# Feed-forward layers of a three-layer transformer on one core: eight block products per step replaced by seven, with the block sums made on GpSimd

## What is computed

```
def swiglu(x, w_gate, w_up, w_down):
    return (jax.nn.silu(x @ w_gate) * (x @ w_up)) @ w_down
x = x + 0.5 * swiglu(rms_norm(x, ffn1_norm), w_gate, w_up, w_down)   # 1024 -> 2816 (2752 in layer 3) -> 1024
x = x + mixer(rms_norm(x, mix_norm))     # pool + latent attention, gated convolution, Fourier + attention
x = x + 0.5 * swiglu(rms_norm(x, ffn2_norm), ...)
```

## Time and profile before

| | us |
|---|---|
| median of 3 runs | 2809.5 (2809.46 to 2810.23) |
| the profiled execution | 2811.45 |
| its span, first to last instruction | 2809.6 |
| PE busy | 2766.3 (98%) |
| DVE busy | 1331.8 (47%) |
| ACT busy | 908.2 (32%) |
| POOL busy | 130.3 (5%) |

### The profile page before, as it was taken

The page is one execution under the profiler, slowest core; times in us unless marked ns, Lnnn a source line. Parts: engine busy times, 40 slices in busy tenths (PEclk is TensorE's granted clock), DMA queues, the critical chain, the costliest instruction groups (busy, mean ns, idle before and its releaser), DMA issues.

```text
span 2809.6 us, 31389 instructions
## 1 busy us (share of the span) xinstructions
PE 2766.3 (98%) x12580; PEld 2261.5 (80%) x12580; DVE 1331.8 (47%) x1895; ACT 908.2 (32%) x1286; POOL 130.3 (5%) x130
## 2 busy tenths in 40 slices
PE   8999999999999999999999999999999999999998
PEld 6888878888888888888888888888877877788776
DVE  5444358654443444434654444344443557544432
ACT  4222226542322223222233232223222346432221
POOL 0000005300000000000000000000000114000000
PEclk9999999999999999999999999999999999999999
DMA  4332232033323333333333333333322320233322
GB/s 152 99 98 91 91 86 77 24 89 103 95 92 96 96 98 90 101 96 96 98 90 98 98 90 98 92 95 91 105 85 89 92 81 23 61 103 100 90 84 70
DMA packets 282704, 253.30 MB, mean 90 GB/s; under 512 B 8384, under 2 KB 278848, under 8 KB 282560
## 3 DMA queue, kind: packets, MB, share of 16 engines
q1 hardware_dynamic: 282560, 251.30, 29.9%
HBM read 249.17 MB, written 2.10 MB: 89 GB/s over the span
## 4 chain that ended last, share of the span: by engine, by line
PE 82%; issue 13%; DVE 3%; ACT 2%; DMA 0%; SPq 0%; POOLq 0%; POOL 0%; DVEq 0%
PE bank L380 27%; PE bank L381 27%; PE bank L382 27%; PE bank L469 1%; DVE a_mx L1235 0%; PE bank L433 0%; PE bank L422 0%; DMA raw<-in_ffn_w_gate 0%; DVE wl L1126 0%; ACT Xh L804 0%; DVE a_nb L1142 0%; ACT wh L773 0%; DVE a_KT L1138 0%; ACT a_P L857 0%; DVE X L1135 0%
## 5 line engine op out<-in xcount | busy, mean ns | idle before, releaser
L1126 DVE TENSOR_TENSOR wl<-raw,wh 128x1024 fp32r<-128x1024 f32 (+6 forms) x498 | 573.9, 1166 | 976.2 <-ACT wh L773 975.3
L380 PE MATMUL bank<-Xh,wl 128*128 128x512 f32 x2544 | 997.6, 392 | 12.9 <-DVE wl L1126 10.6
L382 PE MATMUL bank<-Xh,wh 128*128 128x512 f32 x2544 | 992.0, 390 | 0.0
L381 PE MATMUL bank<-Xl,wh 128*128 128x512 f32 x2544 | 991.5, 390 | 0.0
L773 ACT ACTIVATE wh<-raw 128x1024 fp32r<-128x1024 f32 (+6 forms) x498 | 494.9, 1009 | 1001.3 <-PE bank L382 994.9
L380 PEld LDWEIGHTS bank<-Xh,wl 128*128 128x128 f32 x2544 | 476.3, 187 | 117.0 <-issue 12.6
L381 PEld LDWEIGHTS bank<-Xl,wh 128*128 128x128 f32 x2544 | 476.4, 187 | 102.9 <-issue 1.9
L382 PEld LDWEIGHTS bank<-Xh,wh 128*128 128x128 f32 x2544 | 476.1, 187 | 103.0
L380 PE MATMUL bank<-Hh,wl 128*128 128x512 f32 x1056 | 419.0, 397 | 0.0
L382 PE MATMUL bank<-Hh,wh 128*128 128x512 f32 x1056 | 417.0, 395 | 0.0
L381 PE MATMUL bank<-Hl,wh 128*128 128x512 f32 x1056 | 417.0, 395 | 0.0
(11 more groups left out here) (264 smaller groups left out, 1583.5 us busy)
## 6 DMA issues: line engine op xcount, KB each, us to landing
raw<-in_ffn_w_gate SPq DMA_DIRECT2D x128, 512.0 KB, 3.8
raw<-in_ffn_w_up SPq DMA_DIRECT2D x128, 512.0 KB, 3.9
raw<-in_ffn_w_down SPq DMA_DIRECT2D x114, 512.0 KB, 3.5
raw<-in_c_w_in SPq DMA_DIRECT2D x24, 512.0 KB, 3.7
raw<-in_w_in SPq DMA_DIRECT2D x10, 512.0 KB, 3.8
raw<-in_a_w_in SPq DMA_DIRECT2D x8, 512.0 KB, 3.8
raw<-in_a_w_out SPq DMA_DIRECT2D x8, 512.0 KB, 3.5
raw<-in_c_w_out SPq DMA_DIRECT2D x8, 512.0 KB, 3.5
```

Source lines behind the costliest of these rows:

```text
L380: e.matmul(o, ll, rh, start=start, stop=False)
L381: e.matmul(o, lh, rl, start=False, stop=False)
L382: i = e.matmul(o, lh, rh, start=False, stop=stop)
L1126: e.tensor_tensor(lo, src, hi.bitcast(F), ALU.subtract).then_inc(wlo.up(("w", n)), 1)
```

## The change

Each of an FFN's two matrix products becomes a product of 2x2 blocks, and the eight block products of that are replaced by seven (the Winograd form of Strassen's scheme). For gate and up of one group the blocks of the weights are A11, A12 (gate, upper and lower half of the depth) and A21, A22 (up); the blocks of x are depth halves by token halves. For the down projection they are output halves by the two tiles of each group.

- Weights: per job four blocks are loaded into slots 0 to 8 of `raw` (two slots for each but A11), and GpSimd makes S1 = A21+A22, S2 = S1-A11, S3 = A11-A21 and S4 = A12-S2 in float32. Seven operands are then split as before, with the same two chunks ahead and three buffers.
- x: GpSimd makes the sums T1 to T4 of the normed gain times x (ya, yb, which ScalarE writes), and they are split into XT (T4 into the halves of Xh and Xl that are no longer used). h: VectorE makes its four sums, seven operands of h per group are kept in HO.
- Products: 7 per job, each with 256 moving columns. Their PSUM sums are partly copied out by ScalarE (snapA, snapC, snapU) between products into the same bank, and added up by VectorE and GpSimd.
- Group 0 stays as it was (gate and up with 512 columns). The other ten groups are "up" jobs. HO has room for four groups, so the down projection is made in four phases of 2, 3, 3 and 3 groups, two jobs each, between the up jobs: JOBS gives the order. An up job's products have 4 depth tiles each, those of a down job 2 or 3.
- The weights of layer 3's FFNs are padded from 2752 to 2816. Buffers of the mixers move in SBUF to make room; `rb` and `acc` are single now.

The core of the diff:

```diff
+JOBS = (("up", 1), ("up", 2), ("down", 0, 0), ("down", 0, 1), ("up", 3), ("up", 4), ("up", 5), ("down", 1, 0),
+        ("down", 1, 1), ("up", 6), ("up", 7), ("up", 8), ("down", 2, 0), ("down", 2, 1), ("up", 9), ("up", 10),
+        ("down", 3, 0), ("down", 3, 1))
+PRODUCTS = (("a", "B11"), ("c", "T1"), ("a", "T2"), ("b", "B21"), ("a", "T3"), ("c", "B22"), ("a", "T4"))
...
 # tensor_program
+            def job(s, i):
+                ks = range(4) if up else PHASES[kind[1]]
+                for q, (role, operand) in enumerate(PRODUCTS):
+                    n, h, l, _ = chunk()
+                    fresh = q in (0, 1, 3)
+                    if not fresh:
+                        w.wait_ge(act, ("snap", s, i, {2: 0, 4: 2, 5: 1, 6: 4}[q]))
...
+                    for at, k in enumerate(ks):
+                        for m in range(2):
+                            e.matmul(o, l[:, at, sl], xh, start=start, stop=False, skip_group_check=True)
+                            e.matmul(o, h[:, at, sl], xl, start=False, stop=False, skip_group_check=True)
+                            ins = e.matmul(o, h[:, at, sl], xh, start=False, stop=last, skip_group_check=True)
+                    ins.then_inc(mm.up(("product", s, i, q), ("used", n)), 1)
...
 # scalar_program, one job
+                    use()
+                    finish(i - 1, 0)
+                    snap(i, 0)
+                    use()
+                    finish(i - 1, 1)
...
+                    snap(i, 1)
+                    use()
+                    snap(i, 2)
+                    use()
+                    use()
+                    snap(i, 4)
+                    use()
+                    if up:
+                        silu(i, 0)
+                    use()
+                    if up:
+                        silu(i, 1)
...
 # vector_program, one job; finish of an up job: last_product, use, second_half, h_low(B11) | use, h_sums, h_low
+                    finish(i - 1, 0)
+                    finish(i - 1, 1)
...
+                    use(2)
+                    left(i)
+                    use(2)
+                    right(i)
+                    use()
...
 # gpsimd_program, the start of an FFN and one job
+                tt(a1, a2, a1, ALU.subtract, ("xt", s, "T1"))
...
+                tt(b1, b1, b2, ALU.subtract, ("xt", s, "T4"))
+                norm(s)
+                sums(0)
+                third_sum(0)
...
+                for i, job in enumerate(JOBS):
+                    fourth_sum(i)
+                    if i < LAST:
+                        sums(i + 1)
+                    if job[0] == "up":
+                        scaled(i, 0)
+                    if i < LAST:
+                        third_sum(i + 1)
+                    w.wait_ge(act, ("snap", s, i, 4))
+                    if job[0] == "up":
+                        tt(snapC[:, :, :], snapA[:, :, :], snapC[:, :, :], ALU.add, ("high", s, i))
+                        scaled(i, 1)
```

More of the change, by code:

```diff
@@ new lines, in build, with job_banks, group_before, two @@
+        T4 = G[:, :, :].rearrange("p f (t n) -> p (f t) n", t=2)
+        def job_banks(i):
+            return {"a": 0, "b": 2, "c": 1} if i % 2 == 0 else {"a": 4, "b": 6, "c": 5}
+        UP_LAST = max(i for i, job in enumerate(JOBS) if job[0] == "up")
+        def group_before(i):
+            return max([0] + [job[1] for job in JOBS[:i] if job[0] == "up"])
+        def two(ap):
+            return ap.rearrange("p (a b) -> p a b", a=2)
+        scope(at_Xh)
+        aVh, aVl = (sb(n, [128, 4, T], R) for n in ("a_Vh", "a_Vl"))
@@ L231, in build @@
+        aP3 = [sb(f"a_P{i}", [128, T], F) for i in range(3)]
+        assert place[0] <= at_XT
+        scope(at_XT)
+        aqtm, aktm = (sb(n, [128, 4, 8, 96], F) for n in ("a_qtm", "a_ktm"))
         scope()
+        aCh, aCl = (sb(n, [128, KT, T], R) for n in ("a_Ch", "a_Cl"))
         aRB = sb("a_RB", [128, 10, T], R)
@@ L457, in token_major @@
+            def ffn(s):
+                hooks = [nothing, *stats(s, 7, 7)]
+                for side, b in (("gate", 0), ("up", 2)):
+                    proj([(b + m, (side, s, m)) for m in range(2)], [128, 128], KT, Xh, Xl, x_ready(s), hooks)
+                mm.also(("plain", s))
+                for i in range(len(JOBS)):
+                    job(s, i)
             def token_major(b, name, srcs, h, l, width, n=None):
@@ L844, in ffn, with snap @@
-                residual(s, nt, gain)
+                gain = FFN[s]
+                def snap(i, q):
+                    w.wait_ge(mm, ("product", s, i, q))
+                    if q == 0 and i > 0:
+                        w.wait_ge(pool, ("high", s, i - 1))
+                    elif q == 1 and i > 0:
+                        w.wait_ge(*((dve, ("h", s, i - 1)) if JOBS[i - 1][0] == "up" else (pool, ("high", s, i - 1))))
+                    elif q == 2 and i > 0:
+                        w.wait_ge(dve, ("right", s, i - 1))
+                    elif q == 4:
+                        w.wait_ge(dve, ("left", s, i))
+                    dst = {0: snapA, 1: snapC, 2: snapU, 4: snapA}[q]
+                    copy(dst[:, :, :], two(banks[job_banks(i)["c" if q == 1 else "a"]][:, :]), ("snap", s, i, q),
+                         scale=1.0 if JOBS[i][0] == "up" else 0.5)
@@ new lines, in right @@
+                def right(i):
+                    c = two(banks[job_banks(i)["c"]][:, :])
+                    w.wait_ge(mm, ("product", s, i, 5))
+                    w.wait_ge(act, ("snap", s, i, 2))
+                    if JOBS[i][0] == "up":
+                        dst = G[:, :, 256:512]
+                        tt(dst, c, snapU[:, :, :], ALU.add, ("right", s, i), ("read", ("c", s, i)))
+                        w.wait_ge(dve, HERE)
+                        tt(dst, dst, r2(1), ALU.mult, ("g", s, i, 1))
+                    else:
+                        t = 2 * JOBS[i][2]
+                        dst = X[:, t:t + 2, 256:512]
+                        stt(dst, c, 0.5, dst, ALU.mult, ALU.add, ("read", ("c", s, i)))
+                        w.wait_ge(dve, HERE)
+                        tt(dst, dst, snapU[:, :, :], ALU.add, ("right", s, i), ("x", s, t), ("x", s, t + 1))
@@ new lines, in r2, with last_product @@
+                def r2(t):
+                    return bc(rb[:, 256 * t:256 * t + 256], 1, [128, 2, 256])
+                def last_product(i):
+                    a4 = two(banks[job_banks(i)["a"]][:, :])
+                    w.wait_ge(mm, ("product", s, i, 6))
+                    if JOBS[i][0] == "up":
+                        w.wait_ge(pool, ("s", s, i, 0))
+                        tt(S[:, :, 0:256], a4, S[:, :, 0:256], ALU.mult, ("h1", s, i), ("read", ("a", s, i)))
+                    else:
+                        t = 4 + 2 * JOBS[i][2]
+                        dst = X[:, t:t + 2, 0:256]
+                        stt(dst, a4, 0.5, dst, ALU.mult, ALU.add, ("read", ("a", s, i)), ("x", s, t), ("x", s, t + 1))
@@ L1839, in sync_program @@
             e.dma_start(par[:, :], a["par"]).then_inc(par_in.sem, 16)
-            for n in range(2, len(stream)):
-                fetch(n)
+            for load in stream.loads[2:]:
+                fetch(load)
             for t in range(KT):
```

610 lines of the change are left out of this document (441 added, 169 removed).

## The result

The changed kernel takes 3541.2 us (median of 4 runs, 3540.1 to 3546.1) against 2809.9 for the kernel before beside it (2809.5 to 2812.2): a ratio of 1.260 with a 95% interval of 1.258 to 1.263. It is slower, as forecast, 141 us above the forecast of 3400 and inside the stated 3020 to 3600. The profiled execution of after has a span of 3544.3 us.

What follows compares the result with a forecast made beforehand. Turns between VectorE's two-SBUF-input instructions and GpSimd's sums, worsened by engine order, were taken to bound it: 463 us an FFN against 364.5, 592 more in six on 2811.5, so 3400 us, range 3020 to 3600.

Steps and rivals of the forecast that it cites:

- TensorE alone: TensorE's matmuls in one changed FFN sum to 335 us, 29 less than 364.5, if nothing else is late.
- Each engine fits alone: In an up job VectorE needs 15 us, ScalarE 13 and GpSimd 13.5, each under TensorE's 20.2.
- The turns: VectorE instructions with two SBUF inputs and GpSimd additions exclude each other for their whole length: 25.5 us an up job.
- The walk: Step-by-step order of an up job behind an up job: 28.6 us, TensorE standing 8.3 ahead of product 4; chance 0.48.
- Rival 2: TensorE's clock also halves for 3.5 us after each pause, losing 1.5 us in 66 places: + 99, 3500; chance 0.17.
- Job 16: A down job in each FFN's last phase, costed like any first down job at 24.6 us.
- Second down jobs: The second down job of a phase, walked by the same steps: 17 us, or 14 in phase 0.
- The start: Start of an FFN: TensorE pauses 6.4 us at the diagonal, group 0 ends at 28, job 0 at about 65 us.
- Up jobs behind a down job: Three up jobs an FFN with no h chain, near their turns and TensorE: 22 us each.
- Rival 1: Turns stay full and the order's waits fall into them: 409 us an FFN, 3080 in all; chance 0.20.
- rival 3: Slower still, from handoffs between four engines, 0.05 us in some 20 steps a job, and late loads: 3600 and more; 0.05.
- rival 4: Faster: long GpSimd additions leave VectorE gaps or the lock is short, so TensorE bounds again: 2700; chance 0.08.

Runs made afterwards that it cites:

- e1: Changed kernel with GpSimd's weight sums cut to 32 elements a partition, from the third job of each FFN (S3 and S4 in all jobs): 2889.6 us.
- e2: Changed kernel with weight splits of all jobs but each FFN's first reading a PSUM bank as second input in place of SBUF: 3358.1 us.
- e3: Changed kernel with 56 (or 40) extra unread TensorE matmuls ahead of product 4 of each job behind an up job: 3507.2 us.
- e4: Changed kernel with the h sums, their splits and ScalarE's h copies moved behind those of operands 4 and 5, except for job 16: 3440.6 us.
- e11: Changed kernel with GpSimd's weight sums covering half their elements (S1 and S2 from the third job, S3 and S4 in all): 3185.2 us.
- e8: Changed kernel with job 16 on TensorE reading group 9 twice in place of groups 9 and 10: 3506.8 us.
- e6: Changed kernel with the norm's power on GpSimd ahead of its four x sums in place of behind them: 3524.3 us.

## Why the prediction came out as it did

**TensorE alone, 335 us an FFN: right.** Up jobs of 20.2 us are there once TensorE waits for nobody (e1). In the changed kernel it never set the time.

**Each engine fits alone: right, and no help.** VectorE's 15 us are well under 20.2, yet with the full sums beside it an up job behind an up job goes from 20.2 (e1) to 29.8.

**The turns, all of a sum's length: right.** The signs named for it are there: splits of 3437 ns at the longest (2.26 + 1.14 = 3.4), 1.22 where they meet nothing, X at 680. GpSimd's sums of 1024 took 2.34 to 3.40 us against 2.4 to 3.6. e2 shows that it is the second SBUF input. The mean of 1.57 us in place of "near 2" shows that fewer splits and more h sums met one than I thought. The Trainium skill's price (GPSIMD Engine Reference, "Performance versus the Vector engine"), 2.25 us as an estimate for 1024, is below the shortest of 240, 2.337, so my 2.4 was the better one.

**The walk, 28.6 us: right for the whole job.** Its middle step, four h sums alternating with the fourth sum, S1 and S2 in 8.3 us, is the timeline above, 889.09 to 895.98 with two shorter sums. The pause that it gave as 8.3 us is 6.0 to 8.7. With the clock held up (e3) the job takes 28.1. The order as a cause of its own is shown by e4. One step of it isn't borne out: the walk had 3 us of slack, 17.2 us without GpSimd against TensorE's 20.2, and in e11 half of the sums still cost half of the time. The kernel's time as a whole lies above the 3200 to 3460 given to the walk alone; it is inside the stated range because that took in the clock.

**Rival 2, the clock, at 99 us: right too, and the forecast should have carried it.** It was put beside the walk as another case, with 0.17, while nothing in it excludes the walk: they add. Of the walk 5.8 us are two products that run right behind the pause. e3 measures 90 us. The price of 1.5 us a pause was 1.7 and 1.9, and its sign, a granted clock under 0.95, is there with 0.885. Of the 66 places, 11 an FFN, the text names ten, the jobs behind an up job; job 16 among them has no pause ahead of product 4.

**Job 16: the term that was missing.** It was costed as any first down job, 24.6 us. But PHASES gives the last phase group 10, which job 15 has just made, where the other phases leave out the newest. Its products wait for the whole h chain: 31.3 us, 25.2 without that (e8), so 36 us in all. The lists in front of the prediction said so; it was not read off them.

**Second down jobs: under-sized.** 19.7 in place of 17 us, 3 x 2.7 x 6 = 49 us. Jobs 8 and 13 take 20.1 and 20.0, with a pause of 3.7 us ahead of product 6 that I hadn't walked; they take 15.4 when splits meet nothing (e2), so there it is turns of splits with sums. Job 17 takes 19.0, and still 18.4 in e2 and 18.0 in e1, so its part is something else, which was not taken apart. Up jobs behind a down job were over-sized by as much as 1.2 x 3 x 6 = 22 us.

**The start: right in kind, off in size.** In stage 7 the pause at the diagonal was 9.75 us, not 6.4 (in the three FFNs behind a mixer TensorE stood 6.0 to 6.4 us there), group 0 ended after 36 us, not 28, part of it at half clock, and job 0 ended at 72, not 65, with the stage's end in it: 4 us against the 68 of the sum, 25 us in all. The power's place, which I named as the cause, is worth 17 us (e6), as the x sums, S1 to S3 and the h chain behind it are late by themselves.

The sum by these measures: 3403 + 90 (clock) + 36 (job 16) + 49 - 22 + 25 = 3581, 35 above the profiled execution's 3546. That sum counts something twice: without the clock's part (e3) an up job behind an up job is 28.1, not 28.6, and a first down 23.2, not 24.6, so the walk had 36 x 0.5 + 12 x 1.4 = 35 us too many, which the clock's 90 then fills. Straight from the table, after's stage 7 is 25 us longer than the forecast's, 151 in six stages, and that gives 3554, within 8 us. That the over-sized jobs hid some 57 us (22 + 35) of what was missing is luck. Rival 1 (full turns, 3080) fell since e4 shows that order costs time of its own; rival 3 fell with e1, whose up jobs take TensorE's own 20.2 us with all handoffs and loads in place; rival 4 fell with e1 and e2. What makes up the 2.1 us between the shared 25.5 and e4's 27.6 was not taken apart.

## What to carry to other kernels

Sums moved to an idle GpSimd are not free work beside a VectorE at half load: count the time in which either engine uses two SBUF inputs, as one resource, and compare that with the bound; VectorE does in 1.14 us what holds it up for 2.26. Then read the orders for places where several such instructions become ready together ahead of one that the bounding engine waits for. Where that makes TensorE stand for some microseconds, add the half-clock time behind each pause to the forecast and don't keep it as a rival; and look in the job table for a consumer that needs what the job just before it made.

## What was not expected of the hardware

A VectorE operation with one of its two inputs in PSUM is wholly untouched by GpSimd: of the 714 splits of e2, 335 had a GpSimd instruction beside them, and the longest took 1.226 us. The same for GpSimd: 48 sums of 1024 in e2 that met only such instructions took 2.401 to 2.421 us.

The clock stayed at 0.51 for a stretch of 3.4 us in which TensorE was busy all the time, behind a pause of 7 us, and came back after it: what the clock adds to a pause lies in the work behind it. Time at half clock is 817 us in all, against 638 us in the four rows of TensorE's waits above, yet keeping TensorE busy in its pauses gave back only 90 us of it (e3).
